# Residual from the normalised turns: eight groups of transposes taken out, one GpSimd multiply put in

## What is computed

```python
mods = jnp.split(c_act @ w_ada[l] + b_ada[l], N_MOD, axis=-1)
sh1, sc1, g1, sh2, sc2, g2, sh3, sc3, g3 = mods
h = modulate(rmsnorm(x, norm_g[l, 0]), sh1, sc1)
x = x + 0.5 * g1[:, None, :] * swiglu(h, w_ffn1_in[l], w_ffn1_out[l])
h = modulate(rmsnorm(x, norm_g[l, 1]), sh2, sc2)
...
x = x + g2[:, None, :] * mixed
h = modulate(rmsnorm(x, norm_g[l, 2]), sh3, sc3)
x = x + 0.5 * g3[:, None, :] * swiglu(h, w_ffn2_in[l], w_ffn2_out[l])
```

## Time and profile before

| | us |
|---|---|
| median of 3 runs | 1064.85 |
| lowest, highest | 1064.68, 1065.95 |
| the profiled execution, its own time | 1065.81 |
| its span in the profile | 1064.0 |

### The profile page before, as it was taken

The page is one execution under the profiler, slowest core; times in us unless marked ns, Lnnn a source line. Parts: engine busy times, 40 slices in busy tenths (PEclk is TensorE's granted clock), DMA queues, the critical chain, the costliest instruction groups (busy, mean ns, idle before and its releaser), DMA issues.

```text
span 1064.0 us, 12561 instructions
## 1 busy us (share of the span) xinstructions
PE 1045.2 (98%) x5028; PEld 862.4 (81%) x5028; DVE 584.1 (55%) x673; ACT 393.6 (37%) x436; POOL 41.9 (4%) x31
## 2 busy tenths in 40 slices
PE   5999999999999999999999999999999999999998
PEld 3788888888888888888788898888888888888886
DVE  6896555554755689467677649873222232333323
ACT  4654242332323255363425773452121211323231
POOL 0000000000000060010000000510000000000000
PEclk9999999999999999999999999999999999999999
DMA  9657645555446422422120031313323223232312
GB/s 326 236 200 276 221 172 197 197 177 218 159 162 232 162 80 80 110 89 79 40 71 30 2 80 41 102 57 119 118 79 101 96 85 112 79 119 79 118 41 79
DMA packets 93738, 133.50 MB, mean 125 GB/s; under 512 B 10721, under 2 KB 77149, under 8 KB 93574
## 3 DMA queue, kind: packets, MB, share of 16 engines
q1 hardware_dynamic: 93374, 130.83, 36.7%
q10 hardware_dynamic: 328, 2.17, 0.5%
HBM read 130.88 MB, written 4.21 MB: 127 GB/s over the span
## 4 chain that ended last, share of the span: by engine, by line
PE 96%; DVE 2%; DMA 1%; ACT 1%; issue 0%; SPq 0%; DVEq 0%; ACTq 0%
PE bank L1731 27%; PE bank L1732 26%; PE bank L1733 26%; PE bank L2057 2%; PE bank L2160 2%; PE bank L2253 1%; PE bank L2146 1%; PE bank L1871 1%; PE bank L1865 1%; PE bank L1879 1%; PE bank L2135 1%; DMA x_nat<-in_x 1%; PE bank L1816 1%; PE bank L2236 1%; DVE tmod L1165 1%; DVE h_lo L1171 0%
## 5 line engine op out<-in xcount | busy, mean ns | idle before, releaser
L1731 PE MATMUL bank<-h_hi,w_hi 128*128 128x512 f32 x880 | 345.6, 393 | 0.1
L1733 PE MATMUL bank<-h_hi,w_lo 128*128 128x512 f32 x880 | 342.6, 389 | 0.0
L1732 PE MATMUL bank<-h_lo,w_hi 128*128 128x512 f32 x880 | 342.5, 389 | 0.0
L1091 DVE TENSOR_TENSOR w_lo<-w_raw,w_hi 128x2048 fp32r<-128x2048 f32 x81 | 186.7, 2305 | 282.1 <-ACT w_hi L666 282.1
L666 ACT ACTIVATE w_hi<-w_raw 128x2048 fp32r<-128x2048 f32 x81 | 155.2, 1916 | 495.6 <-PE bank L1733 490.4
L1731 PEld LDWEIGHTS bank<-h_hi,w_hi 128*128 128x128 f32 x880 | 165.2, 188 | 36.7 <-issue 2.1
L1733 PEld LDWEIGHTS bank<-h_hi,w_lo 128*128 128x128 f32 x880 | 165.2, 188 | 34.7
L1732 PEld LDWEIGHTS bank<-h_lo,w_hi 128*128 128x128 f32 x880 | 165.3, 188 | 33.8 <-issue 0.5
L1731 PE MATMUL bank<-a_hi,w_hi 128*128 128x512 f32 x352 | 137.6, 391 | 0.0
L1733 PE MATMUL bank<-a_hi,w_lo 128*128 128x512 f32 x352 | 137.0, 389 | 0.0
L1732 PE MATMUL bank<-a_lo,w_hi 128*128 128x512 f32 x352 | 137.0, 389 | 0.0
(11 more groups left out here) (263 smaller groups left out, 940.1 us busy)
## 6 DMA issues: line engine op xcount, KB each, us to landing
w_raw<-in_w_ffn_in SPq DMA_DIRECT2D x42, 1024.0 KB, 5.1
ada<-in_w_ada SPq DMA_DIRECT2D x28, 1024.0 KB, 5.1
w_raw<-in_w_ffn_out SPq DMA_DIRECT2D x22, 1024.0 KB, 5.0
w_raw<-in_w_mix_in SPq DMA_DIRECT2D x11, 1024.0 KB, 5.3
shift_in<-in_w_ada SPq DMA_DIRECT2D x4, 1024.0 KB, 9.0
scale_in<-in_w_ada SPq DMA_DIRECT2D x4, 512.0 KB, 7.4
x_nat<-in_x SPq DMA_DIRECT2D x2, 1024.0 KB, 8.9
scale_half<-in_w_ada SPq DMA_DIRECT2D x2, 1024.0 KB, 11.6
```

The source lines that it names most:

```text
L1091: ve.tensor_tensor(w_lo[n % 2][:], src[:], as_f32(w_hi[n % 2][:]), ALU.subtract).then_inc(wlo_done, 1)
L1731: te.matmul(out_ap, wh, xh, start=first, stop=False)
L1732: te.matmul(out_ap, wh, xl, start=False, stop=False)
L1733: return te.matmul(out_ap, wl, xh, start=False, stop=last)
```

## The change

`turn_x` and its 32 transposes are taken out. `evac_x(d)` now copies the bank with the turned tile of `xn` to `xT`, so that `xT` first holds the normalised rows; `first_t(d)` reads `xT` and no longer the bank. PE spreads the root mean squares over the partitions in bank 2 with four `matmul`s (eight instructions), ACT copies them to `rms_b` (128 x 512), and POOL multiplies all of `xT` (128 x 4096) by it in one instruction, once all eight `first_t` are done. ACT's order changes: `first_t` of tiles 0 and 1 comes after the copy of `rms_b`, 2 and 3 after all `evac_x`, and 4 to 7 after `whi(3)`, ahead of `shifted_hi(4)`. PE waits for the copy of `rms_b` ahead of `hi_hi(1, range(4))`, since bank 2 is needed there.

```diff
@@ gpsimd
+            pool.wait_ge(rms_spread, 2)
+            pool.wait_ge(first_tmod, DT)
+            nc.gpsimd.tensor_tensor(xT[:], xT[:], rms_b[:].unsqueeze(1).to_broadcast([P, DT, TOK]), ALU.mult
+                                    ).then_inc(rms_spread, 1)
+            pool.wait_ge(rms_spread, 3)
@@ scalar
             def evac_x(d):
-                a.wait_ge(x_tr, d + 1)
-                sc.activation(xT[:, d, :], bank[X_BANK[d]][:], ACT.Copy).then_inc(xT_act, 1)
+
+                a.wait_ge(norms[0].lo, d + 1)
+                sc.activation(xT[:, d, :], bank[XN_BANK[d]][:], ACT.Copy).then_inc(xT_act, 1)
...
             def first_t(d):
 
-                a.wait_ge(norms[0].lo, d + 1)
-                sc.activation(tmod[:, d, :], bank[XN_BANK[d]][:], ACT.Copy, scale=fac[:, 0, d:d + 1]
-                              ).then_inc(norms[0].t, 1)
+                a.wait_ge(xT_act, d + 1)
+                sc.activation(tmod[:, d, :], xT[:, d, :], ACT.Copy, scale=fac[:, 0, d:d + 1]).then_inc(first_tmod, 1)
...
+            a.wait_ge(rms_spread, 1)
+            a.wait_ge(norms[0].rt, 2)
+            sc.activation(rms_b[:], bank[2][:], ACT.Copy).then_inc(rms_spread, 1)
             evac_x(2)
+            evac_x(3)
+            first_t(0)
+            first_t(1)
+            first_hi(4)
+            first_hi(5)
+            evac_x(4)
+            first_hi(6)
+            evac_x(5)
+            first_hi(7)
+            evac_x(6)
+            evac_x(7)
             first_t(2)
             first_t(3)
...
             whi(3)
+            for d in range(4, DT):
+                first_t(d)
             a.wait_ge(shift_out, 2)
             for d in range(4, DT):
                 shifted_hi(d)
-            for d in range(5, DT):
-                evac_x(d)
@@ vector, ahead of the first update of xT
+                if not f.r:
+                    v.wait_ge(rms_spread, 3)
@@ tensor
-            pe.wait_ge(x_loaded[0], 16)
-            turn(bank[1], x_nat, 0, (0, 1))
-            pe.wait_ge(c_step, 2)
-            turn(bank[2], x_nat, 1, (0, 1))
-            pe.wait_ge(x_loaded[1], 16)
-            turn(bank[1], x_nat, 0, (2, 3)).then_inc(x_tr, 1)
-            turn(bank[2], x_nat, 1, (2, 3)).then_inc(x_tr, 1)
-
             pe.wait_ge(bias_consts, 48)
             pe.wait_ge(vec_step, 2)
             te.matmul(bank[3][0:QH, :], relb[:], table[:], start=True, stop=True).then_inc(bias_mm, 1)
             te.matmul(bank[0][:, 0:QH], ones[0:1, :], sink_r[:], start=True, stop=True).then_inc(sink_step, 1)
+            pe.wait_ge(norms[0].rt, 1)
+            pe.wait_ge(c_step, 2)
+            for t in range(TT):
+                ins = te.matmul(bank[2][:, t * P:(t + 1) * P], rms0[:, 1, t:t + 1].to_broadcast([P, P]), ident[:],
+                                start=True, stop=True)
+            ins.then_inc(rms_spread, 1)
...
+            pe.wait_ge(xT_act, 1)
+            turn_xn(3)
             column_sums(16, quarter_acc[1], 2, 2)
-            pe.wait_ge(norms[0].t, 1)
-            turn_xn(3)
-            pe.wait_ge(norms[0].t, 2)
-            turn_x(2)
...
-            pe.wait_ge(xT_act, 2)
+            pe.wait_ge(rms_spread, 2)
             pe.wait_ge(rowpad_done, 1)
             pe.wait_ge(whi_done, 1)
...
-            turn_x(3)
-            turn_x(4)
...
-            turn_x(5)
-            turn_x(6)
...
-            turn_x(7)
```

More of the change, by code:

```diff
@@ L190, in build @@
     table = at("table", [NB + 1, ROW], f32, o_ada + 16 * KB)
+    rms_b = at("rms_b", [P, TOK], f32, region + 64 * KB)
     rows = at("rows", [P, P], f32, region + 82 * KB + 512)
@@ L280, in build @@
         vec_step = sem("vec_step")
-        x_tr, xT_act = sem("x_tr"), sem("xT_act")
+        rms_spread, xT_act = sem("rms_spread"), sem("xT_act")
         xsq_done, xn_done, xn_tr = (sem(n) for n in ("xsq_done", "xn_done", "xn_tr"))
@@ L323, in build @@
         fac_done = [sem(f"fac_done{r}") for r in range(3)]
+        first_tmod = norms[0].t
         class Ffn:
@@ L409, in halves @@
             return ap.rearrange("p (n two b) -> p n two b", two=2, b=b)
-        X_BANK = (1, 2, 5, 6, 4, 6, 4, 5)
         XN_BANK = (4, 5, 6, 4, 5, 6, 4, 5)
@@ L699, in first_t @@
             def first_t(d):
-                a.wait_ge(norms[0].lo, d + 1)
-                sc.activation(tmod[:, d, :], bank[XN_BANK[d]][:], ACT.Copy, scale=fac[:, 0, d:d + 1]
-                              ).then_inc(norms[0].t, 1)
+                a.wait_ge(xT_act, d + 1)
+                sc.activation(tmod[:, d, :], xT[:, d, :], ACT.Copy, scale=fac[:, 0, d:d + 1]).then_inc(first_tmod, 1)
             def shifted_hi(d):
+                a.wait_ge(first_tmod, d + 1)
                 sc.activation(h_hi[:, d, :], tmod[:, d, :], ACT.Identity, bias=modv[:, d:d + 1]).then_inc(norms[0].hi, 1)
@@ L717, in _ @@
             sc.activation(sink_b[:], bank[0][:, 0:QH], ACT.Copy).then_inc(sink_step, 1)
-            evac_x(0)
             a.wait_ge(first_ready[6], 16)
@@ L722, in _ @@
             first_hi(1)
-            first_t(0)
-            first_t(1)
+            evac_x(0)
+            evac_x(1)
             a.wait_ge(bias_mm, 1)
             sc.activation(row8[:], bank[3][0:QH, :], ACT.Copy).then_inc(rowpad_done, 1)
-            evac_x(1)
             first_hi(2)
@@ L1817, in turn @@
                 return ins
-            def turn_x(d):
-                turn(bank[X_BANK[d]], x_nat, d).then_inc(x_tr, 1)
             def turn_xn(d):
@@ L1883, in _ @@
             pe.wait_ge(sink_step, 2)
-            pe.wait_ge(xT_act, 1)
             pe.wait_ge(first_split, 1)
@@ L1902, in _ @@
             hi_lo(1, range(4))
-            pe.wait_ge(xT_act, 3)
+            pe.wait_ge(xT_act, 2)
             turn_xn(4)
-            pe.wait_ge(norms[0].t, 4)
-            turn_x(3)
-            turn_x(4)
             pe.wait_ge(wlo_done, 1)
@@ L1911, in _ @@
             lo_hi(1, (2, 3)).then_inc(first_used, 1)
-            pe.wait_ge(xT_act, 5)
+            pe.wait_ge(xT_act, 3)
             turn_xn(5)
+            pe.wait_ge(xT_act, 4)
             turn_xn(6)
@@ L1917, in _ @@
                 if tiles[0] == 6:
-                    pe.wait_ge(norms[0].t, 5)
+                    pe.wait_ge(xT_act, 5)
                     turn_xn(7)
@@ L1925, in _ @@
             hi_hi(1, (4, 5))
-            pe.wait_ge(norms[0].t, 7)
-            turn_x(5)
-            turn_x(6)
             lo_hi(1, (4, 5))
@@ L1931, in _ @@
             hi_lo(1, (4, 5))
-            pe.wait_ge(norms[0].t, 8)
-            turn_x(7)
             hi_hi(1, (6, 7))
```

## The result

The changed kernel takes 1073.35 us (median of 4 runs, 1072.33 to 1074.63), the kernel before 1064.78 (4 runs). The ratio is 1.0079, with a 95% interval from 1.0067 to 1.0091: 8.6 us slower. The profiled execution of the changed kernel took 1073.66 us with a span of 1071.9, 7.9 us longer than the span before.

What follows compares the result with a forecast made beforehand. PE, busy for 98% of the span, was taken as the bound. With DVE held by POOL, `stage_k8` starts at 68.15 + 5.9 + 1.7 + 0.7 = 76.45, not 66.71: 1064.85 + 9.7 = 1074.5 us, range 1068.0 to 1077.0.

Steps and rivals of the forecast that it cites:

- A: Likeliest path, chance 0.44: POOL's multiply gets in before `shifted_lo(3)`; `stage_k8` starts 9.7 us later, 1074.5 us.
- rival B: POOL asks just after `shifted_lo(3)` has begun; `stage_k8` 7.0 us late, about 0.6 for the clock: 1072.5 us; chance 0.34.
- Who is shut out: Beside POOL's multiply: a DVE instruction with two inputs from SBUF waits for the whole POOL instruction.
- The multiply's length: POOL's multiply of 128x4096 takes 9.2 us, lower bound 7.2, upper bound 10.5.
- When POOL starts: After ACT's four `first_t`, at T + 5.4 = 58.25 + d, asking while `shifted_lo(2)` runs, by 0.1 us.
- T: The end of the second piece on PE, forecast at 52.8 + d us.
- d: Delay of the first `h_hi` from the spread at PE's start: 0.7 us taken, range 0 to 1.6.
- The clock after the stall: After PE's idle time ahead of `stage_k8`: granted clock falls to half, 1.7 us added in A.
- The hidden wait for `rms_b`: PE's wait for ACT's copy is hidden by 0.6 us of PE work: 0 taken, bound 1.1 us.
- The wait at `column_sums(32)`: PE comes at 47.94 + d, DVE's shift steps end at 48.14 + d: 0.3 us of the gain lost.
- Rival D: The multiply shuts nobody out and lies beside PE work; 1.2 us gain is left, 1063.6 us; chance 0.12.
- Rival C: POOL starts over 6 us later than its inputs allow; 3.6 us stall, 1067.7 us; chance 0.07.

Runs made afterwards that it cites:

- late multiply: The changed kernel with the same single POOL multiply started only once 14 pieces of `w_lo` are made, some 110 us later: 1065.37 us against 1064.75, ratio 1.0006.
- earlier start: The changed kernel with ACT's `first_t(4)` to `(7)` ahead of `whi(3)`, so that POOL may start earlier: 1076.26 us against 1064.94, ratio 1.0109.
- fill: The changed kernel with the multiply 110 us later and three POOL fills of unused memory in its old place: 1065.59 us against 1064.94, ratio 1.0009.
- later spread: The changed kernel with the spread moved from PE's start to behind `turn_xn(3)`, ahead of `column_sums(16)`: 1071.36 us against 1064.94, ratio 1.0061.
- late pieces: The changed kernel with the multiply in eight late pieces, the spread still at the start of PE's order: 1065.36 us against 1064.44, ratio 1.0008.
- both mended: The changed kernel with the spread behind `turn_xn(3)` and the multiply in eight pieces, each following one `w_lo` from the twelfth on: 1063.44 us against 1064.94, ratio 0.9986.
- the half: The changed kernel with the multiply in two halves of 128x2048, the second 110 us later: 1069.31 us against 1064.75, ratio 1.0039.
- the pieces: The changed kernel with the multiply as eight instructions of 128x512 in the old place: 1071.18 us against 1064.75, ratio 1.0062.
- second product alone: The kernel before plus one unused POOL product of 128x4096, released when `shifted_lo(2)` is done (`DT + 3`): 1071.78 us against 1064.44, ratio 1.0073.
- first product alone: The kernel before plus one unused POOL product of 128x4096, released when `shifted_lo(1)` is done (`DT + 2`): 1074.55 us against 1064.75, ratio 1.0094.

## Why the prediction was right, and where it was off

The time lay in the range (1068.0 to 1077.0), 1.15 us under the 1074.5 forecast, on the side forecast with 0.88. The path held likeliest, A, did not occur; its rival B did, and the range was wide enough for both. By its steps:

- **Who is shut out** was right, and it carries the result: the two rows of `u_lo` and `a_lo` were enough. The late multiply, the earlier start, the fill, the later spread and the late pieces came out inside the range that the lock gives, both mended 0.04 us above it, the half, the pieces and the second product alone within 0.6 us of it; the first product alone held another tile than its text said, and is explained by that. Every rival named fails in at least one run: the change itself without POOL (the late multiply, the product alone), a shared pace (the pieces, and one `shifted_lo` of 9.30 us among five that keep theirs), POOL's length or end alone (the second product, the earlier start), any POOL work at all (the fill).
- **The multiply's length**: 9.2 us forecast, 9.25 measured. `k_sum`, with two streamed inputs, was the right neighbour, not the product with the broadcast factor (7.2). The 9.25 begins 0.46 us before `shifted_lo(3)` ends; where no such instruction was running, the same size took 8.85 us (the product alone, from 57.36), and 8.88 where one had 0.2 us left (the earlier start). The estimate from "GPSIMD Engine Reference" of the Trainium skill (section 3.1), 9.0 us, lies between.
- **When POOL starts** is the step that failed. I had it ask while `shifted_lo(2)` ran, 0.1 us ahead of `(3)`; it came at 60.41, and `(3)` had begun at 60.13. The second piece ended at 54.89 and not at 54.56 (T with the measured d), which is 0.3 us of it; ACT's copies and `first_t` took the 5.3 us forecast (54.93 to 60.26), and POOL began 0.15 us after them. So rival B took place and not A, on the margin that the prediction called a coin's throw.
- **d, the delay of the start**, is 1.76 us in this execution, not 0.7: `relb` was waited for until 14.31, the upper case (1.6). In the six traces of the experiments with the spread at the start PE waits for `relb` until 12.8 to 13.8 us, and the first `h_hi` comes at 19.25 to 19.88, so d is 0.1 to 0.8 there. The guess of 0.7 was fair for most executions; it was no bound.
- **B's size**: with the measured d, B puts `w_lo` at 74.8 and `stage_k8` 0.6 us behind it, 75.4. The trace has 74.44, 0.4 us less since POOL got in while `(3)` was still running, and 0.6 less since the clock cost nothing there. In the traces the loss is 7.7 us at `stage_k8` and 7.9 in the span. The 8.6 us between the medians lie 0.7 higher because the traced execution of the kernel before was 1.0 us above its median and that of the changed kernel 0.3. That B's 7.6 comes so close is in part luck.
- **A's size**: the first product alone cost 9.8 us, near A's 9.7, but that is no test of A: it held `(2)` and not `(3)`, and had neither the removed turns nor d. One term of A shows in it. PE's 28 matmuls after the stall took 7.92 us (66.81 to 74.73), at 0.228 each 6.4, so the half clock cost 1.5 us, 1.7 forecast.
- **The clock after the stall**: granted at half in the changed kernel, as said, but at nearly no cost, since PE's last eight matmuls ran behind DVE anyway and it was back at 1.00 from 74 us, when `stage_k8` began. (The row is a window of one us: busy time of PE, its weight loads, DVE, ACT and POOL; 0.50 is the granted clock, that is 1.2 and not 2.4 GHz.)

```profile
71.00:72.00 1.00, 1.00 (x4) 0.76 (x4) 1.00 (x2) 0.00 (x0) 0.00 (x0) 0.50 0.00 0
```

- **The clock before 33 us** was left out of the sum, as if it were the same in both kernels, and it is not. Between PE's matmul at 27.09 and the start of the third piece at 54.53 the traced kernel before took 27.44 us, part of it at half clock. The two products alone, with the same PE instructions, took 26.18 us both times, with 1.00 granted from 27 to 36 us. The kernels with the change took 25.9 (changed), 25.7 (late multiply), 26.6 (fill) and 26.6 (late pieces), all with a part at half clock, the last two with a longer one. Set against the kernel before at full clock, the five turns taken out (2.2 us of PE's work) bring 0.3 to 0.5 us there or lose 0.4, before d is counted. One window from the first product alone, then from the late pieces:

```profile
28.00:29.00 1.00, 1.00 (x6) 0.83 (x5) 1.00 (x2) 1.00 (x1) 0.00 (x0) 1.00 1.07 391
```

```profile
28.00:29.00 1.00, 1.00 (x4) 0.81 (x3) 1.00 (x3) 1.00 (x1) 0.00 (x0) 0.50 1.05 385
```

The executions of the experiments can be told apart by their mean granted clock. The kernel before stands in them with 51 executions on three chips, so rows differ in the chip as well. Means of the times in us, number of executions in brackets:

| kernel | clock 1.000 | 0.998 | 0.997 |
|---|---|---|---|
| before, three chips | 1064.24 (29) | 1065.31 (22) | none |
| late multiply | none | 1064.74 (6) | 1066.12 (5) |
| fill, late multiply | none | 1065.08 (3) | 1065.78 (7) |
| late pieces | none | 1064.80 (6) | 1065.76 (5) |
| both mended | 1063.63 (2) | 1063.38 (8) | 1064.33 (1) |

At 0.998 the kernels with the spread at the start are 0.2 to 0.6 us faster than the kernel before, and both mended is 1.9 us faster. What makes the clock fall more often in the changed kernels is not shown. In the traces of all of them PE stands for 1.22 us before that first matmul, against 0.28 in the kernel before, where a turn of `x_nat` came in between.

- **The hidden wait for `rms_b`** stayed hidden: ACT's copy ended at 32.62, PE came at 33.42. The wait at `column_sums(32)` was 0.30 us; the prediction has 0.3 too, although its own terms (48.14 and 47.94) give 0.2.
- **Rival D** (1063.6 without the lock) is not what a kernel with the spread at the start reaches: the late multiply, which takes the lock out of PE's way, has 1065.4. The size of d alone does not account for it. In the trace of the late pieces d is 0.14 us, and yet `stage_k8` starts at 66.25, only 0.46 us ahead of the kernel before: the stretch with the longer half clock lies between. With the spread moved, 1063.44 is reached.
- **Rival C**, a late first start of POOL, did not occur: POOL began 0.15 us after ACT's last `first_t` (60.26).

## What to carry to other kernels

Work given to an idle GpSimd that reads SBUF is free only if no VectorE instruction with two SBUF inputs that TensorE waits for stands beside it (and a `TENSOR_SCALAR` was held too); look for the longest GpSimd instruction in the trace and at what VectorE did meanwhile, and put the work where VectorE's results are not due. A cut into pieces helps little in the wrong place and is not needed in the right one. And four small matmuls put at the head of a chain that starts by waiting on loads cost 1.9 us between the medians, nearly the 2.2 us of twenty transposes taken out of its dense part: count what is added where the chain starts before counting what is removed. A single trace of the kernel before shows one of the clocks that its executions run at; look at the granted clock of all of them before taking a stretch at half clock as given.

## What was not expected of the hardware

- A GpSimd fill of 9.5 us leaves VectorE's two-input instructions at full pace, where a multiply of 9.25 us stops them. "SBUF — State Buffer" of the Trainium skill (SBUF: two separate sides) says so, in that it counts VectorE instructions with two SBUF inputs as shut out only against a GpSimd operation that reads SBUF; the two rows agree.
- The clock granted to TensorE before 33 us differs between executions of one kernel, and with it the time: 1.1 us between the means of the two groups of the kernel before (0.6, 1.4 and 1.1 us on the three chips).
- The landing of a load of 1 KB (`relb`, waited for until 12.8 us in one execution and 14.3 in another, with the same list of transfers ahead of it) moves the start of the whole chain where the spread stands behind it.
